# First modulation of the first layer in four half blocks instead of two blocks, with the S5 coefficients and power tables moved behind parts of h

## The reference, cut to what matters

```
silu_c, silu_cc = silu(c), silu(c_ctx)
ada_lat = silu_c @ ada_w[l] + ada_b[l]        # 1024 x 6144
ada_ctx = silu_cc @ ada_w[l] + ada_b[l]
sh1, sc1, g1, sh2, sc2, g2 = split(ada_lat, 6)
csh1, csc1, ... = split(ada_ctx, 6)
h  = rms_norm(x, ln1) * (1 + sc1) + sh1
hc = rms_norm(xc, ln1) * (1 + csc1) + csh1
z  = h @ w_in                                  # 12 column tiles of 128
...
a_bar, b_bar = s5_discretize(...)              # the coefficients, powers and tables of the scan
```

## Time and profile before

| | us |
|---|---|
| median of 3 executions | 2121.73 (2119.9 to 2123.04) |
| the profiled execution, its device time | 2121.68 |
| span of the profiled execution | 2119.9 |
| TensorE busy | 2085.3 (98%) |
| VectorE, ScalarE, GpSimd busy | 1174.5, 522.3, 1075.3 |
| first matmul of tile 0 starts at | 28.62 |
| `tile(3)` starts at | 59.55 |

### The profile page before, as it was taken

The page is one execution under the profiler, slowest core; times in us unless marked ns, Lnnn a source line. Parts: engine busy times, 40 slices in busy tenths (PEclk is TensorE's granted clock), DMA queues, the critical chain, the costliest instruction groups (busy, mean ns, idle before and its releaser), DMA issues.

```text
span 2119.9 us, 31214 instructions
## 1 busy us (share of the span) xinstructions
PE 2085.3 (98%) x12276; PEld 1889.1 (89%) x12276; DVE 1174.5 (55%) x2126; ACT 522.3 (25%) x862; POOL 1075.3 (51%) x1224
## 2 busy tenths in 40 slices
PE   6999999999999999999999999999999999999998
PEld 5999999877899999999999999888777788888887
DVE  6987981455653658466575542793266645122223
ACT  4115121454401230211201221412365113010011
POOL 3752453200155375555665644565601566777773
PEclk9999999999999999999999999999999999999999
DMA  7363354233352155443546427355301522322222
GB/s 289 107 141 108 120 204 127 94 120 115 134 185 89 50 188 205 169 174 132 197 135 187 151 85 199 111 179 165 136 26 38 209 95 90 109 95 94 100 100 70
DMA packets 110432, 281.96 MB, mean 133 GB/s; under 512 B 23210, under 2 KB 45098, under 8 KB 108510
## 3 DMA queue, kind: packets, MB, share of 16 engines
q1 hardware_dynamic: 74544, 206.60, 28.5%
q10 hardware_dynamic: 35758, 73.50, 10.7%
HBM read 241.72 MB, written 37.88 MB: 132 GB/s over the span
## 4 chain that ended last, share of the span: by engine, by line
PE 95%; DVE 2%; ACT 1%; POOL 1%; issue 1%; DMA 0%; DVEq 0%; ACTq 0%; POOLq 0%
PE ps L512 68%; PE ps L625 5%; PE ps L1223 3%; PE ps L1097 2%; PE ps L1237 2%; PE ps L647 2%; PE ps L1273 2%; PE ps L651 1%; PE ps L1123 1%; PE ps L1135 1%; PE ps L1170 1%; PE ps L952 1%; PE ps L703 1%; PE ps L1086 1%; PE ps L829 1%
## 5 line engine op out<-in xcount | busy, mean ns | idle before, releaser
L1458 POOL TENSOR_SCALAR whi<-raw 128x1024 fp32r<-128x1024 f32 x244 | 265.8, 1089 | 995.6 <-PE ps L512 486.5
L1462 POOL TENSOR_TENSOR wlo<-raw,whi 128x256 fp32r<-128x256 f32 x732 | 618.9, 873 | 20.4
L512 PE MATMUL ps<-hh,whi 128*128 128x384 f32 (+1 forms) x1512 | 449.7, 353 | 0.0
L512 PE MATMUL ps<-hh,wlo 128*128 128x384 f32 (+1 forms) x1512 | 447.8, 351 | 0.0
L512 PE MATMUL ps<-hl,whi 128*128 128x384 f32 (+1 forms) x1512 | 447.5, 351 | 0.0
L512 PEld LDWEIGHTS ps<-hh,whi 128*128 128x128 f32 x1512 | 275.5, 188 | 19.7 <-issue 1.1
L512 PEld LDWEIGHTS ps<-hh,wlo 128*128 128x128 f32 x1512 | 276.5, 188 | 18.4
L512 PEld LDWEIGHTS ps<-hl,whi 128*128 128x128 f32 x1512 | 276.3, 188 | 18.5 <-issue 0.2
L512 PE MATMUL ps<-midh,whi 128*128 128x384 f32 (+1 forms) x672 | 201.5, 353 | 0.0
L1465 POOL TENSOR_TENSOR wlo<-raw,whi 128x256 fp32r<-128x256 f32 x244 | 201.3, 825 | 0.0
L512 PE MATMUL ps<-midh,wlo 128*128 128x384 f32 (+1 forms) x672 | 200.9, 352 | 0.0
(11 more groups left out here) (303 smaller groups left out, 3396.8 us busy)
## 6 DMA issues: line engine op xcount, KB each, us to landing
raw<-in_w_main SPq DMA_DIRECT2D x244, 512.0 KB, 3.3
dot_w<-in_ada_dot SPq DMA_DIRECT2D x80, 512.0 KB, 4.6
ada_mixer<-in_ada_w SPq DMA_DIRECT2D x24, 512.0 KB, 4.0
g_d<-gt ACTq DMA_DIRECT2D x24, 384.0 KB, 2.3
gl<-g_d ACTq DMA_DIRECT2D x8, 1152.0 KB, 6.2
ada_first<-in_ada_w SPq DMA_DIRECT2D x16, 512.0 KB, 13.9
cout_d<-cz SPq DMA_DIRECT2D x12, 512.0 KB, 5.0
cout<-cout_d ACTq DMA_DIRECT2D x6, 1024.0 KB, 8.5
```

Source lines behind the costliest of these rows:

```text
L512: ins = pe.matmul(bank(p, h, a, b), ww[:, w % W_SLOTS, kw * P:(kw + 1) * P], xx[:, kx, a:b], start=(first and i == 0 and j == 0), stop=(la ...
L1458: pool.tensor_scalar(whi[:, u, :], raw[:, u % 2, :], 1.0, 0.0, ALU.mult, ALU.add).then_inc(w_split.sem, 1)
L1462: pool.tensor_tensor(wlo[:, u, c:c + LO_PART], raw[:, u % 2, c:c + LO_PART], whi[:, u, c:c + LO_PART].bitcast(F32), ALU.subtract)
```

## The change

- The 16 steps become four blocks of 4 steps. Block i gives shift and scale of parts 2i and 2i+1 (`ada_tile` and the layout of `ada_w` are changed to fit). A step holds two groups of 128 inputs, each in its own 32 rows of the sums, and the turn adds the two (`pick_two`). A block has its own turn, copy, bias and gain (`pe_first_turn`, `act_first_rows`, `dve_first`, `first_gain`).
- TensorE: turn 0 comes behind step 3, the spread is no longer interrupted, steps 6 and 7 follow it. In the loop over parts, turns 1, 2, 3 come ahead of parts 1, 3, 5, and steps 8 to 15 ahead of parts 1 to 4, two each. Tile 2 joins at part 6 instead of part 4.
- ScalarE: copies of blocks 1, 2, 3 ahead of `hh` of parts 1, 2, 4; `step_sizes` and `magnitudes` behind part 3, `sines` behind part 5.
- VectorE: two parts after each block; `coefficients` behind part 3, `transition` behind part 5, all of `doubled` behind part 7.
- SyncE: tile 1 is loaded behind step 3 instead of step 7. GpSimd: `wlo` of tiles 0 and 1 in one instruction of 1024 columns; tile 2 waits for `hl` of part 3.

```diff
+        def pe_first(pe, s):
+            i, u = divmod(s, 4)
+            sums = first_home(i)[0]
+            if u == 0 and i >= 2:
+                pe.wait_ge(ada_row.sem, ada_row.at(("first", i - 2)))
+                pe.wait_ge(ada_ready.sem, ada_ready.at(("gain", 0, 0, 2 * (i - 2))))
+            pe.wait_ge(ada_full[s].sem, ada_full[s].at(s))
+            for k in range(2):
+                for j in range(2):
+                    r = 32 * (2 * k + j)
+                    ins = pe.matmul(sums[r:r + 32], svec[:, 2 * u + k, :], ada_first[s][:, 512 * k + 256 * j:512 * k + 256 * j + 256],
+                                    start=(u == 0), stop=(u == 3))
+            ins.then_inc(ada_used.sem, ada_used.mark(("first", s)))
+        def act_first_rows(act, i):
+            sums, rows, _ = first_home(i)
+            act.wait_ge(ada_used.sem, ada_used.at(("first", 4 * i + 3)))
+            if i >= 2:
+                act.wait_ge(ada_turned.sem, ada_turned.at(("first", i - 2)))
+            act.copy(rows, sums).then_inc(ada_row.sem, ada_row.mark(("first", i)))
...
-                for k, steps in ((0, range(8, 11)), (1, range(11, 13)), (2, range(13, 16))):
-                    if k:
-                        first_tiles(range(2), k)
-                    for s in steps:
-                        pe_ada(pe, s)
-                pe.wait_ge(hi_ready.sem, hi_ready.at((0, 1, 3)))
-                for i in range(2):
-                    high_step(pe, i, i, 3, TOK)
-                pe_turn(pe, 1)
...
+                for k in range(1, 6):
+                    if k % 2:
+                        pe_first_turn(pe, (k + 1) // 2)
+                    if k < 5:
+                        for s in range(2 * k + 6, 2 * k + 8):
+                            pe_first(pe, s)
+                    first_tiles(range(2), k)
                 wait_w(pe, 2)
-                pe.wait_ge(ada_ready.sem, ada_ready.at(("gain", 0, 0, 4)))
-                for k in range(4):
+                pe.wait_ge(ada_ready.sem, ada_ready.at(("gain", 0, 0, 6)))
+                for k in range(6):
                     first_tiles((2,), k)
-                for k in range(4, KD):
+                for k in range(6, KD):
                     first_tiles(range(3), k)
...
             for s in range(2):
-                pe_ada(pe, s)
+                pe_first(pe, s)
             pe_first_sums(pe)
-            for s in range(2, 6):
-                pe_ada(pe, s)
+            for s in range(2, 4):
+                pe_first(pe, s)
+            pe_first_turn(pe, 0)
+            for s in range(4, 6):
+                pe_first(pe, s)
             pe_first_spread(pe)
+            for s in range(6, 8):
+                pe_first(pe, s)
...
                 if not t0 and u == 2:
-                    pool.wait_ge(prep_dve.sem, prep_dve.at((0, "power", 2)))
+                    pool.wait_ge(lo_ready.sem, lo_ready.at((0, 1, 3)))
...
-                for k in range(KD // 2):
+                act_hi(act, 0, 1, TOK, 0)
+                act_first_rows(act, 1)
+                act_hi(act, 0, 1, TOK, 1)
+                act_first_rows(act, 2)
+                for k in range(2, 4):
                     act_hi(act, 0, 1, TOK, k)
+                step_sizes(act, 0)
+                magnitudes(act, 0)
+                act_first_rows(act, 3)
                 act.dma_start(s5[0].b_in[:], A["ssm_b"][0]).then_inc(prep_loaded.sem, prep_loaded.mark(0, 16))
-                act_rows(act, 1)
-                for k in range(KD // 2, KD):
+                for k in range(4, 6):
+                    act_hi(act, 0, 1, TOK, k)
+                sines(act, 0)
+                for k in range(6, KD):
                     act_hi(act, 0, 1, TOK, k)
...
-                dve_norm(dve, 0, 1, TOK, 0, KD // 2)
+                for i in range(4):
+                    dve_first(dve, i)
+                    first_gain(dve, i)
+                    dve_norm(dve, 0, 1, TOK, 2 * i, 2 * i + 2)
+                    if i == 1:
+                        coefficients(dve, 0)
+                    if i == 2:
+                        transition(dve, 0)
                 doubled(dve, 0, 1)
                 doubled(dve, 0, 2)
-                dve_ada(dve, 1)
-                first_gain(dve, 1)
-                dve_norm(dve, 0, 1, TOK, KD // 2, KD)
                 doubled(dve, 0, 4)
```

More of the change, by code:

```diff
@@ L119, in ada_tile @@
 def ada_tile(row, k):
-    return (k // 4) * 8 + 4 * row + k % 4 if row < 2 else row * KD + k
+    return (k // 2) * 4 + 2 * row + k % 2 if row < 2 else row * KD + k
 FULL = 4
@@ new lines, in pe_first_turn @@
+        def pe_first_turn(pe, i):
+            _, rows, o = first_home(i)
+            if i == 0:
+                pe.wait_ge(ones_ready.sem, ones_ready.at("pick"))
+            pe.wait_ge(ada_row.sem, ada_row.at(("first", i)))
+            for q in range(2):
+                ins = pe.matmul(o[:, q], rows[:, q * P:(q + 1) * P], pick_two[:, :, :], start=True, stop=True, skip_group_check=True)
+            ins.then_inc(ada_turned.sem, ada_turned.mark(("first", i)))
+        def act_first_rows(act, i):
[4 more added lines that the diff above has]
+            act.copy(rows, sums).then_inc(ada_row.sem, ada_row.mark(("first", i)))
@@ L767, in dve_dots_done @@
             dve.wait_ge(ada_ready.sem, ada_ready.at("dots"))
+            for k in range(0, KD, 2):
+                dve_gain(dve, 1, 0, k, k + 2, 2)
             for k in (0, KD // 2):
-                dve_gain(dve, 1, 0, k, k + KD // 2, 2)
                 dve_gain(dve, 1, 1, k, k + KD // 2, 1)
@@ L1377, in load_ada @@
             def load_ada(step):
-                w, slot = ada_slot(step)
+                if step < 8 * ADA_FIRST:
+                    w, slot = ada_first[step], step
+                else:
+                    w, slot = ada_slot(step)
                 sp.dma_start(w[:], A["ada_w"][step]).then_inc(ada_full[slot].sem, ada_full[slot].mark(step, 16))
@@ L1460, in split @@
                 pool.wait_ge(w_split.sem, i * 8 + (2 * u + 1))
-                for c in range(0, KD * P - LO_PART, LO_PART):
-                    pool.tensor_tensor(wlo[:, u, c:c + LO_PART], raw[:, u % 2, c:c + LO_PART],
-                                       whi[:, u, c:c + LO_PART].bitcast(F32), ALU.subtract)
-                c = KD * P - LO_PART
+                c = KD * P - LO_PART if t0 or u >= 2 else 0
+                for a in range(0, c, LO_PART):
+                    pool.tensor_tensor(wlo[:, u, a:a + LO_PART], raw[:, u % 2, a:a + LO_PART],
+                                       whi[:, u, a:a + LO_PART].bitcast(F32), ALU.subtract)
                 pool.tensor_tensor(wlo[:, u, c:], raw[:, u % 2, c:], whi[:, u, c:].bitcast(F32), ALU.subtract).then_inc(
@@ L2646, in _ @@
             dve.wait_ge(early_in.sem, early_in.at(0))
-            for i in range(2):
+            for i in range(4):
                 first_gain_constant(dve, i)
+            dve.tensor_tensor(pick_two[:, :, :], pick[:, 0:2], pick[:, 2:4], ALU.add).then_inc(
+                ones_ready.sem, ones_ready.mark("pick"))
             for k in range(1, KD):
@@ L2651, in _ @@
             first_invert(dve)
-            coefficients(dve, 0)
-            transition(dve, 0)
-            dve_ada(dve, 0)
-            first_gain(dve, 0)
             for l in range(DEPTH):
```

65 lines of the change are left out of this document (28 added, 37 removed).

## The result

The change makes the kernel slower: 2130.95 us (median of 5 executions, 2129.29 to 2132.28) against 2121.73 (2119.9 to 2123.04), ratio 1.0045 [1.0035, 1.0056]. The profiled execution of the change took 2131.77 with a span of 2129.6, so 9.7 of span more than the one before. I predicted 2126.3 in a range up to 2128.6: the sign was right, but of the 9.2 us I had said 4.6.

A forecast was written before the change was run, and what follows sets the result against it. TensorE was taken as the bound, 95% of the span. Start -1.4, turns +0.9, parts 4 and 5 +0.4, waits +1.7, +3.0, +0.35, less an old 0.32, gave +4.6: 2126.3 us, range 2122.6 to 2128.6.

The forecast's parts named there:

- The start, -1.4: Opening up to VectorE's first `nt`: it starts at about 25.6, 1.4 earlier, with bounds 3.6 and 0.4 earlier.
- Rival C: Start: the pause ahead of turn 0 keeps TensorE slow through the spread; first `nt` 26.6, time 2127.3; chance 0.10.
- Two more turns, +0.9: TensorE's modulation: two turns more than before, at 0.45 each, add 0.9.
- Parts 4 and 5, +0.4: TensorE's parts 4 and 5: run as two tiles and one instead of three, adding 0.4.
- First wait, +1.7: TensorE ahead of part 2: `hh` is queued behind ScalarE's copy of block 2, which waits for step 11; 1.7.
- Second wait, +3.0: TensorE ahead of part 4: coefficients meet GpSimd's split of tile 2 and delay the gain; 3.0, bounds 1.7 and 4.0.
- rival B: Weak contention: coefficients run at 1.76, the wait ahead of part 4 is 1.7, no `hl` wait; 2124.7; chance 0.18.
- Table load: ScalarE ahead of the coefficients: 1.28 by the trace row, without the skill's further drain of about 1.38.
- Third, +0.35: Part 4: `hl` meets GpSimd's split of tile 3, 1.97 for 1.14, of which TensorE sees 0.35.
- Behind `tile(3)`: VectorE's later tables: output table 0 has 2.95 of room, 1.0 of it is used; no cost taken.
- Rival D: Late tables: VectorE falls over 2.95 further behind than TensorE, first kernels wait for table 0; 2127.4 to 2128.5; chance 0.08.
- My own sign of being wrong: Wrong if both waits are absent or under 1 together, `tile(3)` starts before 60, or TensorE waits for VectorE behind it.

The follow-up runs named there:

- e5: The change with turn 0 behind step 5 instead of step 3, so no pause for the copy of block 0; 2129.46 us, ratio 1.0044.
- e2: The change with ScalarE's copies of blocks 2 and 3 behind `hh` of both parts of their pair; 2129.57 us, ratio 1.0039.
- e1: The change with GpSimd's split of tile 2 waiting for the end of the angle reduction instead of `hl` of part 3; 2130.16 us, ratio 1.0043.
- e3: The change with coefficients, exponentials and sines ahead of the first modulation, first power behind the first gain; 2127.59 us, ratio 1.0033.
- e7: The change with block 2 and 3 copies behind their pair's `hh`, coefficients in front, spread ahead of turn 0; 2123.85 us, ratio 1.0013.

## Why the prediction was wrong, step by step

- **The start, -1.4: failed.** It took the rise of the level "where the trace has it", near 24.1, and said the new pause of 0.5 "pulls towards the later end", without a price. The pause was what counted: e5 without it has the first `nt` at 25.05. Rival C, at 0.10, was right about the start (first `nt` 26.6 said, 27.04 measured), and the 0.9 for turn 0 too (0.98). Worth 1.4 of the miss.
- **Two more turns, +0.9: right**, 0.43, 0.44 and 0.37 each. **Parts 4 and 5, +0.4:** about 0.1.
- **First wait, +1.7: right**, 1.51, and e2 shows its cause: the copy ahead of `hh`.
- **Second wait, +3.0: right in mechanism, undersized.** I took 0.5 more for each of five operations, from one row; the operations took 3.2 more in all, and each kind was hit but the last operation. The wait was 3.58. My upper bound was added up wrongly: 0.5 more for each of eight operations in place of five gives 4.5, not 4.0. e1 and e3 give the 1.64 that was said for the case without contention (rival B's 1.7). The Trainium skill (SBUF — State Buffer, the single rule on the shared port pair) has the lock held for the whole instruction; by that the wait grows with GpSimd's instruction and not with VectorE's, and e7 agrees: 2.44 for two operations beside one of 2.39.
- **The clock behind the second wait: not in the sum at all.** Part 4 at the low level cost 1.45. The prediction looked at the clock at the start alone, so this is a term that it put at nothing without a reason.
- **Table load: right to go by the row.** In the change the load starts at 38.44, lasts 1.28 and the exponential starts at 39.73. The further 1.38 of drain that the Trainium skill has (ScalarE: Activation LUTs, What ACT_TABLE_LOAD costs) does not show.
- **Third, +0.35: hidden.** In the change no row waits for `hl` of part 4, since the slow products leave it time; in e1, at the fast level, it is 0.57.
- **Behind `tile(3)`, "no cost taken": failed.** Rival D did not occur: output table 0 is first used 7.29 later, as `tile(3)` is, so its room was enough. My own sign of being wrong did come: TensorE waits for VectorE behind `tile(3)`, at `x`. 1.5 of the 2.4 go with the place of a code fetch, which no rival named, and 0.9 with a longer low level in layer 1, whose cause stays open. The Trainium skill (Advanced Engine Details and Errata, ISA Cache) gives the piece as 16 KB, 256 instructions; the 97 packets of 0.02 MB for 24568 matmuls and weight loads, 253 for each packet, and the semaphore instructions beside them agree with that.

The sum as measured, in spans: start +0.07, waits +1.51 and +3.58, clock +1.45, turns +0.88, the old 0.32 gone, 0.1 of rest, 2.4 behind: 9.7. That is 5.1 more than the +4.6 said: 1.4 is the start, 1.45 the clock of part 4, 2.4 what lies behind `tile(3)`, and 0.6 the contention, less 0.8 that the first wait, the third term and parts 4 and 5 fell short of theirs. The two waits that I had named, and what releases them, were right; what failed is the clock, at both places, and the nothing behind `tile(3)`.

## What to carry to other kernels

A wait's price on TensorE is not its length alone: ask which clock level it leaves behind, at the start of work above all, where 0.59 of waiting cost 2 us up to `tile(3)` in the profile. When small operations of VectorE are moved, look which of GpSimd's long instructions they will meet, since a 24-column operation can last as long as the other's whole instruction. And when a change that adds or removes a few instructions moves the time by a tenth of a per cent far from its place, pad the stream with idle instructions and measure again before you believe in any mechanism: as much can be the position of a code fetch. Take a second profile of the unchanged kernel as well: it was 1.1 us off the first behind `tile(3)`, with nothing changed.
